# Spreading the S5 tap products over the gaps of the RWKV state steps in a hybrid RWKV7/S5/PEER kernel

## The reference

```python
def step(state, inp):                      # RWKV7, one token
    r_t, w_t, k_t, v_t, a_t, b_t = inp
    sa = jnp.einsum('bhij,bhj->bhi', state, a_t)
    state = (state * w_t[:, :, None, :] + sa[..., :, None] * b_t[..., None, :]
             + v_t[..., :, None] * k_t[..., None, :])
    return state, jnp.einsum('bhij,bhj->bhi', state, r_t)
# S5: u -> B u -> complex scan with lambda_bar -> C x + D u -> gelu -> gated unit -> rmsnorm
_, _, x_re, x_im = lax.associative_scan(complex_affine_combine, (ar_seq, ai_seq, bu_re, bu_im), axis=0)
y = (jnp.einsum('sbgp,gcp->bsgc', x_re, c_re) - jnp.einsum('sbgp,gcp->bsgc', x_im, c_im))
y = y + d_skip * u; y = gelu(y); y = y * sigmoid(y @ glu_w + glu_b)
x = x + jnp.concatenate([y_rw, y_s5], axis=-1) @ w_out[l]
```

## Time and profile before

| | |
|---|---|
| timed, three runs | 4293.1, 4296.87, 4303.25 us |
| profiled execution, its own time | 4311.72 us |
| its span | 4310.0 us |
| TensorE busy | 3822.1 us, 89% |
| VectorE busy | 3037.8 us, 70% |
| ScalarE busy | 1386.7 us, 32% |
| mean granted TensorE clock | 0.938 of full speed |

### The profile page before, as it was taken

One profiled execution on the slowest core, in us unless ns is written; L12 is line 12 of the kernel. 1 busy time (PEld: TensorE's weight loads), 2 busy tenths in 40 slices (PEclk: granted clock), 3 DMA queues, 4 the chain that ended last, 5 costly groups with the idle time before them and its releaser, 6 DMA issues. The chain is left out here.

```text
span 4310.0 us, 68355 instructions
## 1 busy us (share of the span) xinstructions
PE 3822.1 (89%) x27802; PEld 3472.2 (81%) x27802; DVE 3037.8 (70%) x5326; ACT 1386.7 (32%) x2125; POOL 870.6 (20%) x593
## 2 busy tenths in 40 slices
PE   6778887799998997999989888779999898899997
PEld 4557765589998997999986776559999898899996
DVE  6446463388888987777775645348988897778776
ACT  3442132233333332333334213233333343233332
POOL 3000000001111334444430000001101223444442
PEclk8889888899999998999999998889999999999998
DMA  4730221257776789999961031126777678999994
GB/s 155 269 120 30 96 69 59 69 159 212 209 214 199 275 302 344 340 339 345 341 246 55 22 125 59 39 78 190 208 208 210 210 277 322 340 341 332 342 341 184
DMA packets 324084, 891.84 MB, mean 207 GB/s; under 512 B 29984, under 2 KB 161184, under 8 KB 316352
## 3 DMA queue, kind: packets, MB, share of 16 engines
q1 hardware_dynamic: 250048, 619.09, 43.5%
q0 software_dynamic: 73728, 268.47, 17.3%
HBM read 754.27 MB, written 133.17 MB: 206 GB/s over the span
## 5 line engine op out<-in xcount | busy, mean ns | idle before, releaser
L212 PE MATMUL peer_ps<-peer_h_high,tile_high 128*128 128x384 f32 (+1 forms) x2304 | 801.0, 348 | 67.0 <-ACT up_act L2199 41.2
L2082 POOL DMA_INDIRECT row<-in_peer_u_rows,row_at x256 | 387.6, 1514 | 2094.1 <-DVE row L2312 1236.8
L212 PE MATMUL peer_ps<-gate_high,tile_high 128*128 128x384 f32 x2048 | 710.5, 347 | 94.3 <-DVE tile_low L205 94.3
L214 PE MATMUL peer_ps<-peer_h_high,tile_low 128*128 128x384 f32 (+1 forms) x2304 | 791.4, 343 | 0.0
L213 PE MATMUL peer_ps<-peer_h_low,tile_high 128*128 128x384 f32 (+1 forms) x2304 | 791.4, 343 | 0.0
L205 DVE TENSOR_TENSOR tile_low<-tile,tile_high 128x1024 fp32r<-128x1024 f32 x544 | 662.7, 1221 | 177.1 <-ACT tile_high L200 171.8
L213 PE MATMUL peer_ps<-gate_low,tile_high 128*128 128x384 f32 x2048 | 705.2, 344 | 0.0
L214 PE MATMUL peer_ps<-gate_high,tile_low 128*128 128x384 f32 x2048 | 704.4, 344 | 0.0
L200 ACT ACTIVATE tile_high<-tile 128x1024 fp32r<-128x1024 f32 x544 | 571.2, 1050 | 1.6 <-DMA tile<-in_peer_wq 1.5
L2082 POOL DMA_INDIRECT row<-in_peer_v,row_at x256 | 449.1, 1754 | 486.1 <-DVE own_sum L2318 442.0
L212 PEld LDWEIGHTS peer_ps<-peer_h_high,tile_high 128*128 128x128 f32 x2304 | 438.0, 190 | 91.3 <-issue 63.8
(11 more groups left out here) (439 smaller groups left out, 5506.5 us busy)
## 6 DMA issues: line engine op xcount, KB each, us to landing
tile<-in_peer_u SPq DMA_DIRECT2D x256, 512.0 KB, 4.2
tile<-in_peer_v SPq DMA_DIRECT2D x256, 512.0 KB, 7.3
acts<-up_act SPq DMA_DIRECT2D x256, 192.0 KB, 4.4
gates<-gates_out SPq DMA_DIRECT2D x24, 2048.0 KB, 9.4
gates_in<-gates SPq DMA_DIRECT2D x32, 1536.0 KB, 15.5
act_in<-acts SPq DMA_DIRECT2D x256, 192.0 KB, 7.5
in_w<-in_w_in SPq DMA_DIRECT2D x36, 512.0 KB, 3.6
tile<-in_peer_wq SPq DMA_DIRECT2D x32, 512.0 KB, 4.7
```

The lines of the kernel that those rows point to most:

```text
L212: pe.matmul(out, wh, mh, start=first, stop=False)
L214: return pe.matmul(out, wl, mh, start=False, stop=last)
L2082: pool.indirect_dma_start(row[n % NROW][:, :], None, table, bass.IndirectOffsetOnAxis(ap=row_at[:, n % ROWS:n % ROWS + 1], axis=0)) \
```

## The change

The taps are taken in another order and at other places; no instruction is added or removed. Each of the six gaps, the one after step 1 among them, now holds four taps and 11 groups of input products (9 in the last gap): two taps, half of the groups, two taps, the other half. The gaps so take the taps of t = 1, 2 and 3. The taps of t = 0 go to the places after the y sums (three), after the head means (two) and after the variances (three). Between the last input product and the y sums there is no tap any more.

```diff
-            groups, each = 4 * 2 * SC, -(-4 * 2 * SC // (NCH - 3))
+            groups, each = 4 * 2 * SC, -(-4 * 2 * SC // (NCH - 2))
             for n in range(1, NCH - 1):
...
                 if n == 1:
                     pe.wait_ge(taps_loaded.sem, taps_loaded.at(16))
-                    taps_of(range(SC, 2 * SC))
-                else:
-                    last = s5_in(range((n - 2) * each, min((n - 1) * each, groups)))
+                for half in range(2):
+                    taps_of(range(SC + 4 * (n - 1) + 2 * half, SC + 4 * (n - 1) + 2 * half + 2))
+                    some = range((n - 1) * each, min(n * each, groups))
+                    last = s5_in(some[len(some) // 2 * half:] if half else some[:len(some) // 2])
             last.then_inc(s_in.sem, 1)
             pe.wait_ge(stepped.sem, stepped.at(NCH - 2))
-            taps_of(range(2 * SC, 3 * SC))
...
-            taps_of(range(3 * SC, 3 * SC + 4))
+            taps_of(range(0, 3))
...
-            taps_of(range(3 * SC + 4, 4 * SC))
+            taps_of(range(3, 5))
...
-            taps_of(range(0, SC))
+            taps_of(range(5, SC))
```

## The result

| | timed runs | median us | ratio to before, 95% interval |
|---|---|---|---|
| before | 18 | 4298.13 | |
| after | 18 (4296.7 to 4322.6) | 4311.11 | 1.0027 [1.0015, 1.0039] |

The change makes the kernel slower by 0.27%, some 12 us (13.0 between the medians, 11.5 between the means). The prediction's likeliest case was no net change (4298), and its own range, 4291 to 4304, was missed. The time is near that of the first rival (4309.7) and lies at the very upper edge of the range of 8 in 10, 4286 to 4311.

What follows compares the result with a forecast made beforehand. TensorE's list was taken to bound the stage up to the last y sum, VectorE behind it. Both layers' +12.8 us less 12.0 gave +0.8, 4298 us on the timed median; own range 4291 to 4304, 8 in 10 4286 to 4311.

Steps and rivals of the forecast that it cites:

- rival 1: First layer's clock fall is absent in most timed runs, leaving only the 12.8 us cost: 4309.7 us, chance 0.24.
- What bounds the stage: TensorE's list sets the time up to the last y sum, then VectorE's chain; taps behind the y sums are hidden.
- The clock: Taps in the gaps keep TensorE's clock at 1.00 in the first layer, step 2 to last y sum: -12.0 us.
- The headline: Whole kernel: both layers' +12.8 us against the first layer's 12.0 us back, net +0.8 us; chance 0.44.
- The eight taps on the path: 24 taps instead of 16 ahead of the last y sum: +3.97 us of pure work in each layer.
- The batches: Ten more tap batches ahead of the last y sum, 0.17 us each for entry and exit: +1.7 us a layer.
- The copies: First y sum waits for ScalarE's first copy, no longer covered by taps: +0.75 us a layer, between 0.6 and 1.0.
- The drain: Each tiling change around the gap taps might drain TensorE, 0.27 us each as upper bound; the row suggested 0.17 a batch.
- The range of the other terms: Behind the y sums: variances between -1.4 and +1.4 us a layer, cold spread and late output products up to +2; taken as 0.

Runs made afterwards that it cites:

- after_again: The changed kernel, unedited, timed and profiled a second time: 4310.12 us, ratio 1.0027 to before.
- one_batch: The changed kernel with each gap's four taps in one batch instead of two: one execution 4314.98 us; step 1 to last y add 38.60 and 38.91 us.
- cover: The changed kernel with its last two taps put behind the last input products: step 1 to last y add 39.83 and 39.82 us.
- moved_unsplit: The kernel before with eight more taps (t = 3) ahead of the y sums in one batch, t = 0 behind, no pairs: 4303.57 us, ratio 1.0016.
- hidden: The kernel before with seven of the eight t = 2 taps moved behind the head means: 4289.03 us, ratio 0.9979; again 4289.55 us, 0.9973.
- pairs16: The kernel before with 16 taps in eight pairs in the first four gaps, none between products and y sums: 4299.77 us, ratio 1.0010.
- before_again: The kernel before, unedited, timed and profiled a second time: ratio 1.0016; step 1 to last y add 45.96 and 32.53 us.

## Why the prediction came out as it did

1. *What bounds the stage* held: TensorE's list up to the last y sum, VectorE behind it. The taps that the change took from behind the y sums were hidden; 7.87 against 7.86 us to L1249, and from L1256 on 17.72 against 17.71 us to L1282.
2. *The clock*: behind the first gap it held at full in all eight stages of kernels with taps in every gap (after and after_again, one_batch, cover, two layers each). But none of them had a pause of 0.5 us among the products, and of the 14 stages with the gaps of before (before, moved_unsplit, hidden) the 12 without one held as well. That the taps hold the clock through such a pause, the step on which the gain rests, is thus neither refuted nor shown. The size of 12.0 us is right where the fall is: 44.25 and 45.96 us are 11.2 and 12.9 above the undisturbed 33.1.
3. *The headline*, no net change, failed at one step: I took the fall in the profile of before as the typical execution, with chance 0.44, though I had set beside it that the timed runs lay 14.9 us lower. Two of four profiles had it, and 19 of 81 timed runs had a clock as low. With a fall in about a quarter of the executions the gain is 12 x 0.25 = 3 us and not 12. That was rival 1, and its condition, fewer than half, is what the timed runs point to; the four profiles alone would leave it open. How many of the 43 runs at 0.942 and more had a fall and a better clock elsewhere can't be told from a mean, nor how many of the 19 had none; the quarter is an estimate from the table.
4. *The eight taps on the path*: forecast 3.97 and their batch, measured 4.00.
5. *The batches* were mis-sized: forecast 0.17 us each, measured 0.35. I had read it from one batch of eight with its neighbours, in which a difference of 0.17 was left over; the products that follow a batch also start slower, and that was not in it. Ten more batches are 3.5 us a layer, not 1.7.
6. *The copies*: forecast 0.75, measured 0.81 us.
7. *The drain* (Trainium skill, "TensorEngine Tiling (Array Packing)", Key Properties): with 0.35 us for an entry and an exit, 0.18 for each change of tiling, the runs lie between my row and the full drain of 0.27 that I had set as the bound. That something is paid at every change of tiling agrees with the page; how much, it does not state.
8. *The range of the other terms*: the variances were 6.02 and 6.99 us, within the bound of 1.4; the spread ran partly cold and cost nothing. The idle time before the variances grew by 0.70 us, not 0.5: between the y sums and them stand 384 columns less (1920 instead of 2304), and not one tap of 320. It is hidden, so nothing hangs on it.

The sum with measured sizes: (4.0 + 3.5 + 0.8) x 2 = 16.6 us, less 3 for the fall, is 13.6 us. By the stages themselves it is 40.93 less 33.06, 7.87 us a layer, so 15.7 less 3 = 12.7 us. Measured are 11.5 and 12.9 between the means and 13.0 and 12.5 between the medians. That rival 1's 4309.7 came so near has luck in it: its cost of 12.8 us was about 3 to 4 too low, and its gain of nothing some 3 too low, and the two cancel.

What stays open is why TensorE stands still at every 128th pass in some stretches, and why for 0.54 and 0.70 us in two executions and for less or nothing in the others. It has no releaser in the trace. In both executions with the fall step 1 had begun at about 502 us, while the other first layers of before began at 505; but one_batch began at 502.42 and lost 0.4 us there at most. No kernel of this study isolates it, and none sets such a pause between the pairs of taps.

## What to carry to other kernels

Before a stall of one profiled execution is bought off, find out how many executions have it: profile the kernel again, or sort the timed runs by their mean clock. Filler work is free only while it lies behind another engine's chain; moved ahead of the point that starts the chain, each microsecond counts, and so does each entry into another shape of matmul. Look first at where TensorE idles ahead of slow small matmuls: filling that place hid the work here and in three of four stages kept the clock for what follows.

## What the runs showed of the hardware

- A batch of 128-row float32 matmuls between 32-row ones cost 0.35 us (entry and exit), shared between the batch and what follows (6.57 against 6.22 us in one gap, 2.2 us for six batches).
- 32-row products with 64x64 steps kept a clock of 2.4 GHz for 18.1 us in six of eight stages of before and lost it in two, both about 1 us after a pause of 0.54 and 0.70 us; a pause of 0.16 us at the same instruction lost nothing. Once lost there it stayed at 1.2 GHz until the full-array taps came, over 20 us. In pairs16, 64x64 y sums lost it after a wait of 0.81 us and had it back 3.4 us later with no full-array matmul between.
- Pauses of TensorE without a releaser, 0.15 to 2.85 us in the output products of before and before_again, stood 128 passes and 128 weight loads apart; what causes them no run shows.
- Sixteen matmuls of two columns with 128x128 weights took 3.73 us at full clock and 6.99 at half. With 3.54 us of idle time ahead of them they took 5.59 to 6.99 us in the eight stages of before; with 0.40 us ahead, 3.73 us in three stages and 5.19 in one.
- The mean clock of a run goes with most of the spread of the times of before: 4315, 4301 and 4292 us in its three classes.
